# A three-layer network kernel: expert results scattered in order of choice, last two blocks added through TensorE, eight split up tiles

## What is computed

```python
def hier_moe(h, w_rg, b_rg, w_re, b_re, w_up, w_down):   # h (512, 1024)
    g_logits = h @ w_rg + b_rg                  # 4 groups
    p_g = softmax(g_logits); g_sel = argmax(g_logits)
    e_in = (h @ w_re + b_re) restricted to the chosen group   # 8 experts
    top_v, top_i = top_k(e_in, 2)
    w2 = softmax(top_v) * p_g[g_sel]            # two shares a token
    out = 0
    for n in range(32):                          # w_up (1024, 512), w_down (256, 1024)
        a, b = split(h @ w_up[n])
        out += share_of(n)[:, None] * ((silu(a) * b) @ w_down[n])
    return out                                   # x + out is the kernel's result
```

## Time and profile before

| | |
|---|---|
| median of 3 runs | 2639.24 us (2638.03 to 2646.51) |
| the profiled execution | 2647.0 us, span 2645.1 us |
| busy share of the span | PE 95%, DVE 60%, ACT 43%, POOL 9% |
| DMA moved | 320.65 MB |
| DMA rate in the 40 slices | 1 to 181 GB/s up to the expert stage, 356 to 388 GB/s in it |

### The profile page before, as it was taken

The page is one execution under the profiler, slowest core; times in us unless marked ns, Lnnn a source line. Parts: engine busy times, 40 slices in busy tenths (PEclk is TensorE's granted clock), DMA queues, the critical chain, the costliest instruction groups (busy, mean ns, idle before and its releaser), DMA issues. The chain is left out here.

```text
span 2645.1 us, 32352 instructions
## 1 busy us (share of the span) xinstructions
PE 2504.0 (95%) x11409; PEld 1909.8 (72%) x11409; DVE 1578.3 (60%) x2383; ACT 1150.0 (43%) x1903; POOL 230.4 (9%) x237
## 2 busy tenths in 40 slices
PE   8999997799999999999999999999999999999995
PEld 6877786677888886766788888678757777666663
DVE  6766445745555535644555553547799655588884
ACT  5433332434444325623444442433432532377773
POOL 0000001000000000000000000355324000111111
PEclk9999998999999999999999999999999998899998
DMA  4321231032333322202233331322202013499995
GB/s 149 107 83 66 96 112 56 28 140 80 95 95 95 127 99 73 72 33 91 89 94 101 98 132 60 107 91 100 81 32 96 1 62 106 181 356 376 388 381 221
DMA packets 196720, 320.65 MB, mean 121 GB/s; under 512 B 16513, under 2 KB 112673, under 8 KB 196609
## 3 DMA queue, kind: packets, MB, share of 16 engines
q1 hardware_dynamic: 191678, 310.71, 34.1%
q0 software_dynamic: 4736, 8.40, 1.0%
q10 hardware_dynamic: 195, 0.06, 0.0%
HBM read 298.43 MB, written 29.10 MB: 124 GB/s over the span
## 5 line engine op out<-in xcount | busy, mean ns | idle before, releaser
L399 PE MATMUL ps<-ffn_parts 128*128 128x512 f32 x1056 | 411.5, 390 | 2.4 <-DVE ffn_parts L394 1.7
L401 PE MATMUL ps<-ffn_parts 128*128 128x512 f32 x1056 | 410.8, 389 | 0.0
L400 PE MATMUL ps<-ffn_parts 128*128 128x512 f32 x1056 | 410.8, 389 | 0.0
L399 PEld LDWEIGHTS ps<-ffn_parts 128*128 128x128 f32 x1056 | 198.2, 188 | 46.7 <-issue 2.6
L394 DVE TENSOR_TENSOR ffn_parts<-ring,ffn_parts 128x1024 fp32r<-128x1024 f32 x132 | 157.8, 1223 | 117.8 <-ACT ffn_parts L2454 107.4
L401 PEld LDWEIGHTS ps<-ffn_parts 128*128 128x128 f32 x1056 | 198.2, 188 | 41.2
L400 PEld LDWEIGHTS ps<-ffn_parts 128*128 128x128 f32 x1056 | 198.3, 188 | 40.7
L394 POOL TENSOR_TENSOR w_lo<-ring,w_hi 128x512 fp32r<-128x512 f32 (+1 forms) x112 | 156.0, 1396 | 726.8 <-ACT w_hi L558 726.3
L2505 DVE SCALAR_TENSOR_TENSOR y_tmp<-ps,pcol,y_tmp 128x511 f32<-128x511 f32 x88 | 61.9, 746 | 213.9 <-ACT y_tmp L2438 213.9
L1012 ACT CAST front_w_hi<-ring 128x512 fp32r<-128x512 f32 x104 | 64.1, 620 | 215.0 <-PE ps L401 215.0
L394 DVE TENSOR_TENSOR front_w_lo<-ring,front_w_hi 128x512 fp32r<-128x512 f32 x104 | 71.6, 689 | 131.4 <-ACT front_w_hi L1012 131.2
(11 more groups left out here) (669 smaller groups left out, 5620.2 us busy)
## 6 DMA issues: line engine op xcount, KB each, us to landing
ring<-in_w_up SPq DMA_DIRECT2D x32, 1536.0 KB
ring<-in_ffn_w_up SPq DMA_DIRECT2D x88, 512.0 KB, 4.9
moe_down<-in_w_down SPq DMA_DIRECT2D x32, 1024.0 KB, 10.8
ring<-in_ab_w_in SPq DMA_DIRECT2D x13, 2048.0 KB, 7.8
ring<-in_w_in SPq DMA_DIRECT2D x11, 2048.0 KB, 7.8
ring<-in_ffn_w_down SPq DMA_DIRECT2D x10, 2048.0 KB, 7.8
ring<-in_w_up SPq DMA_DIRECT2D x32, 512.0 KB, 10.4
ring<-in_c_w_in SPq DMA_DIRECT2D x6, 2048.0 KB, 8.1
```

Source lines behind the costliest of these rows:

```text
L399: nc.tensor.matmul(out, left[0], right[0], start=start, stop=False, **more)
L400: nc.tensor.matmul(out, left[0], right[1], start=False, stop=False, **more)
L401: return nc.tensor.matmul(out, left[1], right[0], start=False, stop=stop, **more)
```

## The change

1. WHOLE goes away: all eight up tiles and all eight tiles of x are split (SPLITS = 4). The two plain products of a block become six fp32r products. SP's two up loads are tiles 0 to 5 (after the third quarter is split) and tiles 6 and 7 (after the fourth).
2. The table of results is now ordered by choice and token (1,024 rows). A second one-hot product, `results`, finds for every slot the row of its choice; POOL writes each block's results there with an indirect DMA (`hand_out`, `scatter`), four steps behind its gather. SP's store is gone. Slots without a choice are out of bounds. In the loop the index column is copied, and the copy is waited for with a count, not with a drain.
3. The last two blocks run are not written out. Their shares are brought to their slots by a one-hot product (`shares_of_slots`), ACT and DVE scale and split their results straight from PSUM (`last_result`, `split_result`), and PE multiplies them with one-hot matrices of slot and token (`slots_of_last`, `mixed`); DVE adds these (`add_mixed`).
4. `combine` is gone: SP fetches the eight tiles of the table with plain DMAs as soon as the scatters of the blocks before the last two have landed and `ring` is free, and DVE adds them (`add_picked`) between its work for the last blocks. `rows_and_shares` is replaced by `shares_of_blocks`, after step 3.

```diff
-                sp.dma_start(router.y_beyond, gnext[0:ROWS, :]...to_broadcast([ROWS, MORE, D])).then_inc(k.param_loaded.sem, 16)
+                sp.dma_start(router.y_rows, gnext[:, :]...to_broadcast([P, 2 * NT, D])).then_inc(k.param_loaded.sem, 16)
...
-WHOLE = 2
-SPLITS = (KD - WHOLE) // 2
-SPLIT_ROWS, WHOLE_ROWS = slice(0, SPLITS), slice(SPLITS, KD // 2)
-X_SPLIT = ((0, NT), (NT, KD - WHOLE))
+SPLITS = KD // 2
+FIRST_ROWS, LAST_ROWS = slice(0, SPLITS - 1), slice(SPLITS - 1, SPLITS)
+X_SPLIT = ((0, NT), (NT, KD))
...
# SP, one step
-                    sp.wait_ge(e.up_split, at_block(n, SPLITS, SPLITS))
-                    load_up(later(n, 2), expert, SPLIT_ROWS, e.up_loaded)
-                if inside(n, -2):
-                    store(later(n, -2))
-                if more:
-                    sp.wait_ge(e.whole_done, at_block(n, 1, 1))
-                    load_up(later(n, 2), expert, WHOLE_ROWS, e.whole_loaded)
+                    sp.wait_ge(e.up_split, at_block(n, SPLITS, SPLITS - 1))
+                    load_up(later(n, 2), expert, FIRST_ROWS, e.up_loaded)
+                if more:
+                    sp.wait_ge(e.up_split, at_block(n, SPLITS, SPLITS))
+                    load_up(later(n, 2), expert, LAST_ROWS, e.last_loaded)
...
# SP, after the last step
+            for t in range(NT):
+                if t % 2 == 0:
+                    sp.wait_ge(*r.ring_free(t // 2 + 1))
+                for s in range(2):
+                    at = s * T + t * P
+                    sp.dma_start(picked[:, 2 * t + s, :], y_dram[at:at + P, :]).then_inc(r.row_picked[2 * t + s], 16)
...
# POOL
+            def hand_out(n):
+                s = side(n)
+                pool.wait_ge(e.y_ready, at_block(n, 1, 1))
+                if not isinstance(n, tuple):
+                    scatter(n, r.result[0:ROWS, n:n + 1])
+                    return
+                nc.gpsimd.tensor_copy(e.slot_result[0:ROWS, s:s + 1], r.result[...]).then_inc(e.result_copied, 1)
+                pool.wait_ge(e.result_copied, at_block(n, 1, 1))
+                nc.gpsimd.sem_inc(e.index_seen, 1)
+                scatter(n, e.slot_result[0:ROWS, s:s + 1])
...
# PE, first
-                for c in range(WHOLE):
-                    last = nc.tensor.matmul(out, e.x_whole[:, s, c, :], up[s][:, KD - WHOLE + c, :], start=(c == 0), stop=False)
-                last.then_inc(e.whole_done, 1)
                 for q in range(SPLITS):
...
# PE, after the last step
+            for t in range(NT - 1):
+                for half in range(2):
+                    mixed(t, 0, half)
+            for half in range(2):
+                pe.wait_ge(*r.results_split(3 + half))
+                mixed(0, 1, half)
+            for t in range(1, NT):
+                for b in ((1,) if t < NT - 1 else (0, 1)):
+                    for half in range(2):
+                        mixed(t, b, half)
...
# ACT and DVE, one step
                     split_up(later(n, 2), 2)
+                    split_up(later(n, 2), 3)
...
# ACT, step of the last block but one
+                if last_but_one(n):
+                    split_hidden(later(n, 1))
+                    last_result(0, n)
+                    last_result(1, later(n, 1))
+                    return
...
# DVE, columns
-                nc.vector.tensor_copy(e.x_whole[:, s, :, :], turned_x(KD - WHOLE, KD))
...
# DVE, after(n)
+                if n == 3:
+                    shares_of_blocks(k, r, dve)
...
# DVE, step of the last block but one
+                    shares_of_slots()
+                    split_hidden(later(n, 1))
+                    split_result(0)
+                    return
...
# DVE, after the last step
-            rows_and_shares(k, r, dve)
+            add_picked(0, (0, 1))
+            add_picked(1, (0,))
+            split_result(1)
+            add_picked(1, (1,))
+            add_picked(2, (0, 1))
+            add_mixed(0)
+            add_picked(3, (0, 1))
+            for t in range(1, NT):
+                add_mixed(t)
```

More of the change, by code:

```diff
@@ L4029, in experts @@
     XB, UB, YB, HB = 0, 2, 4, 6
+    MIXED = (2, 6, 4, 0)
+    tiles = out.rearrange("o (t p) d -> p (o t) d", p=P)
     def side(n):
@@ L4120, in _ @@
             each_block(sp, before, step)
-            store((before, 2, 4))
-            store((before, 3, 4))
-            sp.wait_ge(e.y_ended, 32)
+            for t in range(NT):
[4 more added lines that the diff above has]
+                    sp.dma_start(picked[:, 2 * t + s, :], y_dram[at:at + P, :]).then_inc(r.row_picked[2 * t + s], 16)
+            for t in range(NT):
+                sp.wait_ge(*r.combined(t + 1))
+                sp.dma_start(tiles[:, t, :], k.x[:, t, :]).then_inc(k.param_loaded.sem, 16)
+            sp.wait_ge(*k.param_loaded(16 * NT))
         @block.gpsimd
@@ L4167, in _ @@
             after(3)
-            before = pair_before_last(nc.gpsimd)
-            each_block(pool, before, lambda n: step(n) if isinstance(n, tuple) or n >= 4 else None, lambda n: after(n) if n > 3 else None, STATIC_ROWS)
+            for n in range(4, STATIC_ROWS):
+                step(n)
+                hand_out(n - 4)
+                after(n)
+            before = nc.gpsimd.value_load(r.before_last[0:1, 1:2], min_val=NE // 2 - 4, max_val=NB // 2 - 4)
+            with pool.Fori(STATIC_ROWS // 2 - 2, NB // 2 - 3) as i:
+                with pool.If(i <= before):
+                    for b in range(2):
+                        step((i, 4 + b, 0))
+                        hand_out((i, b, 0))
+            for b in range(2):
+                step((before, 6 + b, 8))
+                hand_out((before, 2 + b, 8))
+            for b in range(2):
+                hand_out((before, 4 + b, 8))
+            free_ring()
             pool.drain()
@@ L4195, in first @@
                     for c in (2 * q, 2 * q + 1):
[L4196 removed]
+                        last = product(nc, out, [x[:, s, c, :] for x in (e.x_hi, e.x_lo)], [w[:, c, :] for w in (e.up_hi, e.up_lo)], c == 0, c == 2 * SPLITS - 1)
                     last.then_inc(e.up_done, 1)
@@ L4257, in in_blocks_beyond, with results @@
                 pe.wait_ge(*r.slotted(3))
+            def results(out, early, late):
+                for t in range(2 * NT):
+                    last = nc.tensor.matmul(out, r.is_slot[:, t, :], early[:, t, :] if t < NT else late[:, t - NT, :], start=(t == 0), stop=(t == 2 * NT - 1), skip_group_check=True)
+                last.then_inc(r.results_found.sem, 1)
             def after(n):
@@ L4261, in after, with shares_of_slots, mixed @@
                     tokens(NBANKS - 1, MORE, in_blocks_beyond, r.token_of_block)
+                    results(k.ps[0:ROWS, NBANKS - 1, MORE:2 * MORE], r.result_of_block, r.result_of_block[:, NT:2 * NT, :])
+            def shares_of_slots():
+                pe.wait_ge(*r.shares_split(1))
+                for t in range(2 * NT):
+                    last = nc.tensor.matmul(k.ps[0:ROWS, XB, 0:4], r.is_slot[:, t, :], r.share_parts[:, t, :], start=(t == 0), stop=(t == 2 * NT - 1))
+                last.then_inc(r.shares_moved.sem, 1)
+            def mixed(t, b, half):
+                out, at = k.ps[:, MIXED[t] + half, :], slice(half * BANK, (half + 1) * BANK)
+                for n, y in enumerate((e.dn_hi, e.dn_lo)):
+                    last = nc.tensor.matmul(out, at_slot(b)[:, t * P:(t + 1) * P], y[0:ROWS, 0, b, at], start=(b == 0 and n == 0), stop=(b == 1 and n == 1),
+                                            skip_group_check=True)
+                if b == 1 and half == 1:
+                    last.then_inc(r.mixed.sem, 1)
             fill_wait(k, NBANKS - 1, 4)
@@ L4330, in result, with last_result @@
                 last.then_inc(e.y_ready, 1)
+            def last_result(b, n):
+                act.wait_ge(*r.shares_read(1))
+                act.wait_ge(e.down_done, at_block(n, 1, 1))
+                for half in range(2):
+                    at = slice(half * BANK, (half + 1) * BANK)
+                    nc.scalar.activation(e.dn_hi[0:ROWS, 0, b, at], k.ps[0:ROWS, (YB, XB)[b] + half, :], ACT.Copy, scale=r.share_of_slot[0:ROWS, b:b + 1]).then_inc(r.results_cast.sem, 1)
             def step(n):
```

202 lines of the change are left out of this document (123 added, 79 removed).

## The result

| | before | after |
|---|---|---|
| median, us (lowest to highest; runs) | 2639.74 (2636.28 to 2646.99; 13) | 2623.58 (2620.53 to 2634.14; 13) |
| profiled execution, us | 2647.0 | 2628.97 |
| its span | 2645.1 | 2627.2 |
| turn of PE in the steady state | 9.494 | 9.186 |
| start of the expert stage (`IOTA` of `moe_falling` on POOL) | 2282.39 | 2282.42 |

The ratio is 0.9939 with a 95% interval of 0.9927 to 0.995: 16.2 us less, against the 16.3 forecast. The profiled pair differs by 17.9 us in span, all of it inside the expert stage, which starts at the same moment in both. From that start to the end of the span is 362.7 us before and 344.8 after; I call this the length of the stage.

The account below looks back on a forecast made before the run. The prediction took PE (TensorE) to set the pace, with the loads just keeping up. Its terms, -10.9 + 1.6 + 3.5 - 10.5 = -16.3 us, took 2639.24 to 2622.9 us, range 2615 to 2635.

Parts of the forecast that it names:

- 0.12 for the DMA engines: Rival: the DMA engines keep a block's turn at 9.51 us, only the tail is won, 2633.3 us; chance 0.12.
- Part 1: All eight up tiles split: PE saves 0.34 us a block, its turn becomes 9.17 us, 10.9 us in all.
- (b): Rival: DVE and ACT wait for each other and spoil 0.2 us a block, 2629 us; chance 0.12.
- (d): Rival: DVE becomes the bound with a turn of 10.6 us, 2668 us; chance 0.06.
- Part 2: Results scattered by POOL instead of stored by SP: less traffic a block, pace stays PE's, cost zero.
- rival (e): POOL's two issues a block hold DVE up for their whole length, turn 10.7 us, 2671 us; chance 0.02.
- Part 3: Work moved into the expert stage: 1.6 us of small products on PE and 3.5 us of stalls from DVE batches.
- step by step: 1.8 late, 2.0, 2.3: DVE's lateness in us over three batches with 0.4 us slack; PE stalls 1.0, 1.2 and 1.5 us.
- The first block: Start of the stage: a fourth quarter on DVE (1.2 us) before `layout` and before ACT's exponentials costs zero.
- Part 4: The tail with plain fetches and DVE alone setting it: ends at X + 23.0 against X + 33.5, 10.5 us saved.
- X: The moment the second product of block 30 ends on PE; the span ended at X + 33.5 before.
- rival (c): The fetches of the tail come late, 2629.4 us; chance 0.08.

Follow-up runs that it names:

- Experiment 1: The kernel before with all eight up tiles split, results still stored and gathered: 2629.7 us, ratio 0.9957 to the kernel before.
- experiment 2: The changed kernel with the last two up tiles as plain fp32 products again, keeping scatter and new tail: 2632.65 us, ratio 0.9972.
- experiment 6: The changed kernel with DVE making `layout` before the four `expert_up_lo` of block 0: 2621.96 us, ratio 0.9917.
- Experiment 3: The changed kernel with `shares_of_blocks` moved from after step 3 to just before the last pair: 2622.52 us, ratio 0.993.
- Experiments 4: The changed kernel with loops cut to 32 experts, so no empty turns are left and no further blocks possible: 2618.26 us, ratio 0.9913.
- experiment 5: The changed kernel with loops ending at the number of pairs read from memory, every number of blocks still possible: 2618.33 us, ratio 0.991.
- experiment 7: The changed kernel with one fetched row set of tile 3 weighted and added on POOL instead of DVE: 2624.85 us, ratio 0.9937.

## Why the prediction was right, and where it was not

**The bound.** Right. I took PE for the pace and kept 0.12 for the DMA engines. Experiment 1 shows a block's traffic of before moved at 400 GB/s in PE's shorter turn. PE's 0.2 us of waits in 260 settle who sets the pace of before, but not whether the DMA engines would at 9.17 us; only experiment 1 settles that. The DMA share, which stands at 1.02 at 383 GB/s and 1.03 at 400, is not a measure of what is left.

**Part 1.** The mechanism is right, the size a tenth too large. The steady turn fell by 9.494 - 9.186 = 0.308 us, not 0.34. Both ends were off: the 9.51 of the earlier trace rows is the longer of two alternating turns (9.48 and 9.51), and the new one is 9.186, not 9.17. Experiment 1 has 9.167, so 0.02 us a block come with the scatter or with what changed beside it; which, isn't settled. In experiment 2, beside the plain products, the scatter adds nothing (9.487 against 9.494). Over 31 turns the 0.308 are 9.5 us, where I had 10.5.
DVE's busy time of 8.5 us a turn (37.2 / 40 x 9.19) is 0.2 under my 8.75, and so its idle time is 0.66 and not 0.4. Its waits for ACT fell to (11.1 + 4.7) / 27 = 0.6 us a block, mine were 0.4. It never held PE in a steady turn, so no row speaks for rivals (b) and (d).

**Part 2.** Right as to the time: the scatter costs nothing that shows, the loads wait for nobody, and the DMA moved 357 to 389 GB/s over stretches of 40 us, around the 372 forecast. The share went up to 1.03 in one stretch and so not always under 1.0. Not foreseen was POOL's issue of 1.65 to 1.91 us when it falls beside `expert_down_lo`. DVE is not lengthened by it (`expert_down_lo` is 2.36 us for two, `expert_up_lo` 1.22 in the mean), so rival (e) is wrong about who pays. `SBUF — State Buffer` of the Trainium skill (section "SBUF: two separate sides") has the later of the two blocked, whichever it is. With DVE first the traces agree in direction: 4.87 against 1.21 us in experiment 6. With POOL first they do not: a split that starts within an issue keeps its 1.22 us. So the length is measured and that it is this lock is not shown; I had set the rule aside on one row of 0.98 us, where POOL was first. The trace of before would have shown the length to me, at the first gather, which I had not taken as a price:

```profile
2293.25 3.48 DVE L394 TENSOR_TENSOR expert_up_lo<-ring,expert_up_hi 128x1024 fp32r<-128x1024 f32 x3
...
2294.34 3.71 POOL L4129 DMA_INDIRECT y_tmp<-normalised_rows,moe_token  x1 [4.66 <-DVE moe_token L3928]
```

The issue takes 3.71 us there beside three splits, which keep their pace. It ends 1.3 us behind the last of them, and so does the one of 4.87 us.

**Part 3.** This is the step whose terms were mis-sized most. Before block 31 I had 3.5 us of stalls and 0.8 of PE's own products; the trace has 1.9 for both. Excess of each turn over the steady one:

| turn | before | after | what it holds |
|---|---|---|---|
| 2 to 3 | 0.02 | 0.01 | nothing |
| 3 to 4 | 0.40 | 0.77 | first batch on DVE |
| 4 to 5 | 0.68 | 1.36 | 8, now 16 small products on PE; second batch |
| 5 to 6 | 0.07 | 0.88 | third batch on DVE |

The difference is 1.85 us. Two things went wrong in the step "step by step: 1.8 late, 2.0, 2.3". The slack was 0.66 a turn and not 0.4. And I added PE's own products and DVE's stall of the same turn, where they lie beside each other: 1.36 is just twice the 0.68 of eight products, and nothing is left for a stall. The waits that PE does show for `expert_x_lo` are 0.55 and 0.62 us, after the first and the third batch:

```profile
2341.03 0.47 PE L399 MATMUL ps<-expert_up_hi,expert_x_hi 128*96 128x512 f32 x1 [0.55 <-DVE expert_x_lo L394]
...
2361.65 0.47 PE L399 MATMUL ps<-expert_up_hi,expert_x_hi 128*96 128x512 f32 x1 [0.62 <-DVE expert_x_lo L394]
```

Experiment 3 takes the third one away and gains its 0.89 us in that turn. Experiments 1 and 2 part the two causes. With the new batches and the old slack (experiment 2) the last three excesses are 0.41, 1.37 and 0.05 us; with the old batches and the new slack (experiment 1) 0.82, 0.69 and 0.00. So a batch costs PE something only once the slack is gone, and the products cost the same either way.

The first block came out at zero, as forecast (-0.15 us), but by luck and not for my reason. The fourth split does cost something: it lengthens the gather's issue by 1.16 us (4.87 less 3.71), so that the gather lands 1.1 us later. PE started block 0 no later for it, because what it does between the gather and block 0 took 4.15 us before, at a granted clock of 0.66 (2300 to 2305), and 2.97 after, at 1.00.

**Part 4.** Right: X + 22.7 against X + 23.0, with DVE alone setting it and the fetches in time, so no row speaks for rival (c) either. The pieces were 0.70 us for a split of 512 columns (I had 0.75), 1.33 an addition from a fetched tile (1.34), 1.16 to 1.22 a mixed one (1.22).
What I missed stands ahead of X. The turn into the last pair is 2.2 to 2.4 us longer than a steady one in both kernels (11.65 and 11.59), while PE waits behind empty turns of the loop. I took it as given and never asked what it was. In the kernel after, the clock falls with it, and the block 31 products cost some 1.6 us more, which is most of the +1.91 against +0.46 in the ledger. Experiments 4 and 5 show the cause, and its price in the stage: 2.4 us of pause and 1.6 of clock (5.3 in the medians).

**The sum.** -16.2 was measured in the medians against -16.3, but the closeness is largely luck: errors of up to 2.4 us to either side cancelled. The errors, against the profiled pair: part 1 +1.0, part 3 before block 31 -2.4, first turns and last turn +0.5 together, block 31 at the slow clock +1.5, tail -0.35, first block -0.15; and -1.7 that I take for no effect of the change: in the profiled execution of before the granted clock stands at 0.91 and 0.75 in 2310 to 2320 and the turn from block 1 to 2 takes 11.18 us, which after doesn't have (1.00, 9.21 us), nor experiment 2 with the plain products of before (9.54).

```profile
2310.00:2315.00 5.00, 3.40 (x16) 1.69 (x14) 4.78 (x8) 4.14 (x7) 3.03 (x4) 0.91 0.40 147
2315.00:2320.00 5.00, 5.00 (x18) 3.22 (x17) 3.22 (x3) 1.79 (x2) 2.32 (x2) 0.75 0.91 301
```

They sum to -1.6, the difference between -17.9 and -16.3. The medians differ by 1.7 us less than the pair (the profiled execution of before was 7.3 us above its median, that of after 5.4), as they would if the last term were gone from them; with one trace of each kernel that is not shown. The +1.5 for the slow clock is of the same kind, since the trace of before is the only one with the pause and without the fall.

## What to carry to other kernels

Where one engine is busy without a gap and waits for nothing, price the change by that engine's own instructions, and ask of the others only whether their work per turn still fits; a DMA share near 1 is no proof that the DMA engines are full. Extra work on a second engine and extra work on the bounding one in the same turn overlapped here (1.36 us with both, 1.37 where DVE's was hidden), so try the larger of the two before their sum. And look at the turn that is longer than its neighbours in the kernel before, even if the change doesn't touch it: here a loop end and the places of two calls brought 6.2 us in the stage (9.7 in the medians) beside the change's 16.2.

## What the runs showed of the hardware

- Turns of a hardware loop that are skipped by a condition cost time: PE stands still 2.2 us ahead of the last pair, and the clock of the products behind it may fall (0.43 us a product instead of 0.23, in six of seven traces). With a register for the loop's end both are gone (experiment 5: 2.4 and 1.6 us).
- An indirect DMA's issue on POOL takes 0.92 to 0.99 us alone (1.21 for the first of the stage), 1.5 to 2.0 when it meets a split on DVE that is already running (3.0 once, with a batch behind the splits), 3.71 beside three running splits, and 4.87 beside four. The splits keep their 1.22 us (2.35 for two). With POOL computing on the same kind of data instead, DVE pays too: 3.99 us became 5.46 and 5.94 (experiment 7).
- DMA moved 400 GB/s over 40 us, loads, gathers and stores together, where 383 had looked like the limit; its share was 1.03 and 1.02 (experiment 1 and before).
